# Five reorderings in a two-network fp32 kernel: a joint norm's mean, a weight split, a block's statistics, bias rows and a gain scaling

## What is computed

```python
def rmsnorm(x, g):
    y = x * lax.rsqrt(jnp.mean(x * x, axis=-1, keepdims=True) + 1e-6)
    return y * g

# first stack: two layers, then the final norm
x = x + even_mixer(rmsnorm(x, ..), ..)        # "even":  stick-breaking and sparse attention
x = x + conv_glu_ffn(rmsnorm(x, ..), ..)      # "conv0": gated MLP with a 3-tap convolution
x = x + odd_mixer(rmsnorm(x, ..), ..)         # "fox":   forgetting attention, 16 heads
x = x + conv_glu_ffn(rmsnorm(x, ..), ..)      # "conv1"
x = rmsnorm(x, final_norm)
# second stack
x = x + 0.5 * _swiglu(_rms(x, ..), ..)        # "glu0"
x = x + _hgrn2(_rms(x, ..), ..)               # "hgrn":  gated linear recurrence
x = x + 0.5 * _swiglu(_rms(x, ..), ..)        # "glu1"
k_pads, v_pads = _shared_kv(x, ..)            # "kv":    keys and values of three groups, keys normed per head
x = x + 0.5 * _swiglu(_rms(x, ..), ..)        # "glu2"
x = x + _dilated_attention(_rms(x, ..), ..)   # "dilated": three dilated groups, relative biases from rel_bias
x = x + 0.5 * _swiglu(_rms(x, ..), ..)        # "glu3"
```

## Time and profile before

| | |
|---|---|
| median of 3 runs | 1957.86 us (1954.37 to 1959.96) |
| profiled execution: time | 1954.76 us |
| profiled execution: span | 1952.7 us |
| TensorE busy | 1894.5 us, 97% of the span |
| VectorE, ScalarE, GpSimd busy | 1195.3, 976.6, 112.6 us (61%, 50%, 6%) |
| DMA | 320.53 MB, mean 164 GB/s |
| TensorE's mean granted clock | 0.994 of full speed |

### The profile page before, as it was taken

One profiled execution on the slowest core, in us unless ns is written; L12 is line 12 of the kernel. 1 busy time (PEld: TensorE's weight loads), 2 busy tenths in 40 slices (PEclk: granted clock), 3 DMA queues, 4 the chain that ended last, 5 costly groups with the idle time before them and its releaser, 6 DMA issues.

```text
span 1952.7 us, 36124 instructions
## 1 busy us (share of the span) xinstructions
PE 1894.5 (97%) x15516; PEld 1811.5 (93%) x15516; DVE 1195.3 (61%) x1387; ACT 976.6 (50%) x1139; POOL 112.6 (6%) x52
## 2 busy tenths in 40 slices
PE   7999999899999989999999999999999998999999
PEld 7879999898999989999999999888999987779999
DVE  7667766655866775558667555533555566647554
ACT  7365444545544454345446343776634456655332
POOL 0000000110000000000000000333000011220000
PEclk9999999999999999999999999999999999999999
DMA  7315454443554445555335554455555546425552
GB/s 272 123 56 187 177 189 155 154 146 104 180 190 168 177 140 204 178 172 176 124 112 194 175 191 172 158 173 174 183 184 181 185 162 178 113 95 194 189 176 104
DMA packets 57977, 320.53 MB, mean 164 GB/s; under 512 B 6144, under 2 KB 19536, under 8 KB 20752
## 3 DMA queue, kind: packets, MB, share of 16 engines
q1 hardware_dynamic: 55968, 314.76, 47.1%
q10 hardware_dynamic: 1904, 4.24, 0.6%
HBM read 317.85 MB, written 1.12 MB: 163 GB/s over the span
## 4 chain that ended last, share of the span: by engine, by line
PE 87%; DVE 7%; ACT 3%; issue 2%; DMA 1%; SPq 0%; DVEq 0%; ACTq 0%
PE bank L396 27%; PE bank L398 26%; PE bank L397 26%; DVE lo L346 2%; ACT hi L340 1%; PE bank L463 1%; PE bank L1905 1%; PE bank L500 1%; PE bank L2256 1%; DVE xl L970 1%; PE bank L481 0%; DMA ring<-in_dq 0%; DVE arena L556 0%; PE bank L1298 0%; DVE x L980 0%
## 5 line engine op out<-in xcount | busy, mean ns | idle before, releaser
L396 PE MATMUL bank<-xh,hi 128*128 128x256 f32 x2960 | 846.9, 286 | 17.5 <-DVE lo L369 9.9
L397 PE MATMUL bank<-xl,hi 128*128 128x256 f32 x2960 | 839.4, 284 | 0.0
L398 PE MATMUL bank<-xh,lo 128*128 128x256 f32 x2960 | 839.2, 283 | 0.0
L346 DVE TENSOR_TENSOR lo<-ring,hi 128x2048 fp32r<-128x2048 f32 x274 | 623.6, 2280 | 304.4 <-ACT hi L340 304.1
L340 ACT ACTIVATE hi<-ring 128x2048 fp32r<-128x2048 f32 x290 | 549.2, 1898 | 418.5 <-PE bank L398 407.4
L396 PEld LDWEIGHTS bank<-xh,hi 128*128 128x128 f32 x2960 | 568.2, 192 | 26.4 <-issue 16.2
L397 PEld LDWEIGHTS bank<-xl,hi 128*128 128x128 f32 x2960 | 568.3, 192 | 2.3 <-issue 1.5
L398 PEld LDWEIGHTS bank<-xh,lo 128*128 128x128 f32 x2960 | 568.2, 192 | 0.5
L396 PE MATMUL bank<-gh,hi 128*128 128x256 f32 x1056 | 300.3, 284 | 9.3 <-DVE gl L900 9.3
L398 PE MATMUL bank<-gh,lo 128*128 128x256 f32 x1056 | 299.3, 283 | 0.0
L397 PE MATMUL bank<-gl,hi 128*128 128x256 f32 x1056 | 299.3, 283 | 0.0
(11 more groups left out here) (256 smaller groups left out, 1863.2 us busy)
## 6 DMA issues: line engine op xcount, KB each, us to landing
ring<-in_ffn_in SPq DMA_DIRECT2D x132, 1024.0 KB, 4.9
ring<-in_ffn_out SPq DMA_DIRECT2D x66, 1024.0 KB, 4.9
ring<-in_kv SPq DMA_DIRECT2D x24, 1024.0 KB, 4.9
ring<-in_hg_in SPq DMA_DIRECT2D x16, 1024.0 KB, 4.8
ring<-in_od_in SPq DMA_DIRECT2D x12, 1024.0 KB, 4.8
ring<-in_dq SPq DMA_DIRECT2D x12, 1024.0 KB, 4.9
ring<-in_ev_in SPq DMA_DIRECT2D x10, 1024.0 KB, 5.1
arena<-rel_rows SPq DMA_DIRECT2D x24, 256.0 KB, 3.6
```

The source lines that it names most:

```text
L346: ns.tensor_tensor(lo[n % RING][:, 0:w], ring[n % RING][:, 0:w], hi[n % RING][:, 0:w].bitcast(F32), ALU.subtract).then_inc(lo_ok[lo_by[n]], 1)
L396: nc.tensor.matmul(out_, lh, rh, start=start, stop=False, **kw)
L397: nc.tensor.matmul(out_, lh, rl, start=False, stop=False, **kw)
L398: return nc.tensor.matmul(out_, ll, rh, start=False, stop=stop, **kw)
```

## The change

It makes five edits, none of which adds or removes an instruction:

1. In glu0 the second mean (L692) is issued inside ff_in(1), between the two halves of its gate chunk, instead of behind ff_in(1).
2. In conv0's last step VectorE splits fox's chunk n0+1 there, ahead of the four residual additions, instead of behind them.
3. In kv the block's statistics are issued between the two token halves of the first value chunk, instead of at the end of chunk 0.
4. In dilated SP issues the first head pair's six bias transfers behind the load of chunk 5 instead of behind that of chunk 4.
5. In dilated VectorE scales the query gains (QG) after the first four take_outs instead of before them.

```diff
-        def ff_in(pe, j, par, n, F, first, it=None):
+        def ff_in(pe, j, par, n, F, first, it=None, between=None):
...
                 for e in range(2):
+                    if between is not None and h == 0 and e == 1:
+                        between(pe)
                     ee = slice(e * P, (e + 1) * P)
...
-            ff_in(pe, 1, 1, n + 2, F, None)
-            if b == FINAL:
-                pe_final_stats(pe)
+            ff_in(pe, 1, 1, n + 2, F, None, None, pe_final_stats if b == FINAL else None)
...
             elif not first:
-                lo_until(dve, m + (5 if par else 4))
+                lo_until(dve, m + (5 if par or b == "conv0" else 4))
...
                     if value:
-                        pe_wide(pe, n0 + c, value_banks(k // 2), k % 2, k % 2 == 0, c == 23, mean if early else None)
+                        pe_wide(pe, n0 + c, value_banks(k // 2), k % 2, k % 2 == 0, c == 23,
+                                mean if early else lambda: pe_stats(pe, "kv"))
...
-                    if c == 0:
-                        pe_stats(pe, "kv")
...
-                for p in {4: [0], 8: [1], 10: [2], 12: [3], 13: [4], 15: [5, 6, 7]}.get(c, []):
+                for p in {5: [0], 8: [1], 10: [2], 12: [3], 13: [4], 15: [5, 6, 7]}.get(c, []):
...
             def dve_part(dve):
+                for c in range(4):
+                    take_out(dve, c)
                 nc.vector.tensor_scalar(QG[:, :], vecs[:, ROW_QG:ROW_QG + 3], DH ** -0.5, None, ALU.mult).then_inc(qg_ok, 1)
                 dve.wait_ge(qg_ok, 1)
-                for c in range(4):
-                    take_out(dve, c)
                 norms(dve, 0)
```

## The result

| | before | after |
|---|---|---|
| median of the runs, us | 1957.3 (1954.37 to 1959.96, 4 runs) | 1940.49 (1939.68 to 1942.25, 4 runs) |
| profiled execution: time, span | 1954.76, 1952.7 | 1942.25, 1940.2 |
| TensorE busy | 1894.5, 97% | 1896.4, 98% |
| mean granted clock, profiled | 0.994 | 0.995 |

The median of before has one run more than ahead of the change, taken beside it. The ratio is 0.992, with a 95% interval of 0.9902 to 0.9938: faster, and 0.5 us from the forecast of 1940.0. But two terms of the sum were off in opposite directions, and the interest is in those.

What follows compares the result with a forecast made beforehand. TensorE, busy 97% of the span, bounds the kernel, so only its waits and clock count. Gains of 8.6 + 2.9 + 1.5 + 4.0 = 17.0 us gave 1937.8 from the profile, 1940.9 from the median; forecast 1940.0, range 1933 to 1947.

Steps and rivals of the forecast that it cites:

- edit 1's term: glu0: the earlier mean removes the 7.2 us wait and slow clock behind it, so ff_in(2) starts 8.6 us earlier.
- next in line: glu0: with gl early, VectorE's scaling of x and split of the next gate chunk limit ff_in(2), at about 712.4.
- the step counted 4.6: fox: behind the gate chain, the first scores' product starts at about 378.3 instead of 382.91, 4.6 us earlier.
- The 1.7 us that I took off for a slow stretch: fox: a remaining wait of some 2.2 us lowers the clock for 3.4 us, costing 1.7 us and leaving 2.9.
- TensorE reaches the first mean at 1238.7 instead of 1241.83 and waits 1.3 us: kv: TensorE arrives earlier but waits for the first keys' squares, leaving a gain of 1.6 us, taken as 1.5.
- the slow stretch behind the old wait: kv: clock at 0.55 over 3.3 us after the 1.4 us wait, 1.5 us that would go with that wait.
- The bound between waits that do and do not lower it: TensorE's clock: a 1.03 us wait in fox left it full, 1.4 in kv lowered it, so the threshold lies between.
- a forecast by that rule: fox, kv, dilated: all three shorter waits lower the clock, leaving 2.9, 0 and 4.0 us, 15.5 us in all.
- Rival D: dilated: the clock stays low through the softmax, up to 5.1 us per stretch, eight giving 1981 us, slower than before; chance 0.02.

Runs made afterwards that it cites:

- constants early: The changed kernel with ScalarE's load of kv's constants issued at the start of glu1, not behind kv's root: 1937.26 us, ratio 0.9896.
- the last kernel: The changed kernel with kv's constants issued by ScalarE directly ahead of the root of the kv statistics, not behind it: 1935.79 us, ratio 0.9904.

## Why the prediction was right, and where it was not

All 14 profiles together, with the stage lengths in us. "Without" and "with" are means over the profiles whose kernel lacks or has the edit:

| stage | without | with | difference | forecast (bounds) |
|---|---|---|---|---|
| fox, edit 2 | 346.0 (6: 345.54 to 346.62) | 340.8 (8: 340.24 to 341.76) | 5.2 | 2.9 (2.5 to 4.9) |
| glu0, edit 1 | 533.2 (6: 532.87 to 533.89) | 524.2 (8: 524.21 to 524.26) | 8.9 | 8.6 (7.2 to 8.8) |
| kv, edit 3 as made | 342.0 (8: 341.56 to 343.20) | 344.4 (3: 343.34, 344.84, 345.02) | -2.4 | 1.5 (-0.3 to 1.6) |
| kv, edit 3, constants early | same | 341.5 (2: 341.48, 341.45) | 0.5 | |
| dilated, edits 4 and 5 | 384.8 (4: 383.07 to 386.5) | 379.6 (7: 377.48 to 381.7) | 5.2 | 4.0 (2.97 to 5.4) |

5.2 + 8.9 - 2.4 + 5.2 = 16.9 us, and the medians differ by 16.8; the forecast sum was 17.0. The total was right because two sizes that were too small (fox above its upper bound) paid for one of the wrong sign. That the sum came within 0.5 us is luck; only edit 1's term was forecast as it came. The 16.9 against 16.8 is closer than such means can be trusted: the kv term rests on three profiles, in two of which the clock fell.

**Edit 1** was right in mechanism and size: the mean at 3.30 us behind L683 as counted, ff_in(2) 18.92 us behind L683 instead of 27.55, that is 8.63 us, and the split as next in line, with 0.28 us of waiting.

**Edit 2** was right in mechanism, its size too small. From conv0's last ff_out to the product behind L1790 it took 34.90 us before and 29.64 after, so 5.3 us where the step counted 4.6: rs_b starts 4.7 us earlier instead of 4.3, and the chain behind it is 0.6 us shorter. Before, ScalarE's L1697 waited 0.59 us for a bank of TensorE and VectorE's L1790 then 0.61 us for ScalarE's L1809; in the changed kernel, with TensorE ahead, neither waits. The wait is 1.65 us, not 2.2. The 1.7 us that I took off for a slow stretch fell due in the changed kernel's profile, but only in 3 of the 8 profiles that have this wait.

**Edit 3** had the wrong sign. The step that failed is "TensorE reaches the first mean at 1238.7 instead of 1241.83 and waits 1.3 us". It followed rs_b, the keys and their squares, and these came as counted: squares done 13.41 us into the stage, 13.6 by the forecast, and with the constants early the wait is 1.22 us. But the mean has a second input, the constant matrix, whose transfer ScalarE issues behind the root of the statistics. I had let the root slip by 1.1 us and not asked what else is issued behind it. In the trace of before that transfer never showed as a wait, since it landed 5 us ahead of its use. The size was wrong too, and early constants do not mend that. Of the 1.6 us forecast, 1.5 was the slow stretch behind the old wait, and the clock fell there in 2 of 8 profiles only. At full clock on both sides the edit is worth 0.1 us with early constants (the 0.5 in the table comes from those two), and costs 1.8 as made (343.34 against 341.57).

**Edits 4 and 5** were right in mechanism: the first wait gone, a tensor_scalar of 0.16 us, the norms 2.8 us ahead of TensorE (3.0 forecast), and the two edits redundant. In the pair of profiles, the scores at 1604.29 come 5.2 us earlier in the stage than those at 1618.53 did (5.3 forecast), and the stage ends 3.5 us earlier. The mean is 5.2, since the wait that they remove was 2.97 us in before's profile but 3.3, 3.6 and 4.1 in the three others without these edits. The one shown was the shortest. Some 0.3 us of the 5.2 come from a later fall of the clock that the profiles have unevenly (see below): 60 us into the stage the means differ by 4.9.

**The clock.** "The bound between waits that do and do not lower it lies somewhere from 1.03 to 1.4 us" is wrong: it made a threshold out of one execution. The same wait, in the same program order, lowers the clock in some executions only. The stretch behind the 1.41 us wait in kv, in the kernels with edit 1 alone and with edits 4 and 5 alone:

```profile
1228.99:1232.29 3.30, 3.30 (x11) 2.59 (x10) 2.51 (x3) 0.63 (x2) 3.30 (x1) 0.61 0.80 217
```

```profile
1236.70:1240.00 3.30, 3.30 (x16) 2.71 (x15) 2.51 (x3) 0.63 (x2) 3.30 (x1) 1.00 0.85 282
```

By such rows it fell in 2 of 8 profiles behind the 1.41 us wait, in 3 of 8 behind the 1.65 us wait, and in 2 of 3 behind the 3.1 to 3.3 us wait, at 1.5 to 1.7 us each time. It is a chance and a price, not a rule. Waits shorter than the 1.03 us of fox did not keep it up either: in the changed kernel's dilated it fell behind two waits of 0.82 and 0.81 us (the score row at 1595.97, 1.38 us long instead of 0.92). The prediction had weighed a rule of the Trainium skill ("TensorE: Matmul & The Clock Gate", section "A second HAM failure mode: psum-queue depth-cycling"), that short idle moments, come often enough, make the clock swing. The runs agree in so far as it does swing, and a forecast by that rule that has every wait paid for would have taken too much off. Rival D, a clock low through dilated's softmax, did not come. But in 6 of the 14 profiles it fell once more 135 to 140 us into that stage, where the forecast had no fall; it cost 1.7 to 1.9 us in five of them and 0.1 in the changed kernel's. Two of the six are of kernels without edits 4 and 5, so it does not come from the change.

**What stays open.** The medians of the single edits do not add up. By their ratios, edit 1, edit 2, edit 3 and edits 4 and 5 are worth 4.7, 2.3, -3.5 and 4.5 us, together 8.0, where the whole change gives 15.7 by its own ratio. The stages that an edit touches do add up. The kernels of edits 1 and 2 alone ran at a mean clock of 0.9915 and 0.990 (medians over their runs), those of before at 0.993 and those of the change at 0.996, and in before's runs 0.001 of clock goes with about 1.2 us. Why programs that differ in one place differ in clock elsewhere was not settled. Nor do the medians rank the last versions: with the constants early or before the root, or edit 3 undone, they lie from 1935.8 to 1939.7 us, all below the changed kernel's 1940.49. They come from different chips; by their ratios to before on the same chip they lie at 0.9893 to 0.9909, against 0.992 for the changed kernel, with overlapping intervals. By the kv stage, the changed kernel with earlier constants is 1.9 us shorter at full clock and also avoids the wait behind which the clock may fall. The lowest median is that of the last kernel, 1935.79, but on the chip on which before is fastest too (1955.38), and its ratio of 0.9904 is not the lowest.

## What to carry to other kernels

When a step moves, list every input of each instruction that follows it, and for inputs that come by DMA list which instruction issues them: a transfer that lands early today shows no wait, and here a slip of 1.1 us in its issue made it land 5 us later, which lengthened the block by 1.9 us. Read a threshold or a price of the clock only from several executions, and compare kernels by stages cut at common instructions rather than by whole spans. If two edits remove the same wait, test each alone: here one was enough.

## What the hardware showed that was not expected

- A 64 KB transfer on ScalarE's queue landed from 1.8 to 6.5 us after its issue, in all 14 profiles 0.2 to 0.7 us behind the 1 MB load of SyncE that was in flight.
- A wait of 3.1 us left TensorE's clock at 1.00 in one execution, where waits of 3.2 and 3.3 at the same place lowered it in two others, and one of 1.41 us lowered it in 2 of 8. Two waits of 0.8 us stood ahead of a fall in dilated.
- The even block, the same in all 14 kernels, took some 3.3 us more in 6 of 14 profiles (351.2 to 351.8 us up to conv0's last ff_out, against 348.0 to 348.6); in the changed kernel's profile the clock is at 0.77 in a stretch there.
- A tensor_scalar on three columns took 2.4 us beside a GpSimd split and 0.16 or 0.17 us without one, while a reciprocal beside the same split took its usual 1.75 us.
